# Two gate projections ahead of the mLSTM query/key projection, and the small loads released by an earlier load

## Chip, cores and metric

One core of one Trainium2 chip. The metric is the time of one execution in microseconds (us), and lower is better. The kernel is written out engine by engine: TensorE (matmuls), VectorE, ScalarE, GpSimd and SyncE each have a list of instructions of their own, and wait for each other on semaphores only.

## The reference, cut to what matters

One step of a two-layer diffusion trunk over 128 context and 256 latent tokens (T = 384), width 1024. The change lies in the first mixer of layer 0:

```
sh1, sc1, g1, sh2, sc2, g2 = split(silu(cvec) @ ada_w[l] + ada_b[l])      # adaLN, 1024 x 6144 per layer
h = rmsnorm(x) * (1 + sc1) + sh1
proj = h @ rec_w_in
qa, ka, va, ra, qb, kb, vb, ob, gk_lr, mg = split(proj)                   # 256 256 512 512 256 256 512 512 32 16
glog = log_sigmoid(gk_lr @ gla_gk_w + gla_gk_b) / 16                      # gates of the GLA heads
ig, lf = mg + mlstm_gate_b                                                # gates of the mLSTM heads
out_a = gla_scan(qa, ka, va, glog, state_gla); out_b = mlstm_scan(qb, kb, vb, ig, log_sigmoid(lf), state_mlstm_*)
x = x + g1 * (concat(norm(out_a) * silu(ra), norm(out_b) * sigmoid(ob)) @ rec_w_out)
```

Behind it follow a mixture of 16 experts, layer 1 (a long convolution, adaLN as well) and a second mixture of experts. All of it is in fp32.

## The kernel before

**Weights.** All large weights pass through `ring`, six slots of 2 MB. SyncE issues the loads of the list `order` one after the other (`load`, L607); a load into a slot first waits until the last use of what was in the slot is over. The order of this stretch: x and the position table (2.5 MB), adaLN loads 0 to 3 of layer 0 (slots 0 to 3), rec_w_in blocks 0, 3, 1, 4 (slots 4, 5, 0, 1), then adaLN loads 4 to 11 alternately in slots 2 and 3, then those of layer 1. A block of rec_w_in gives four query/key products: block 0 is `qka` (query and key of the GLA heads), block 3 `qkb` (those of the mLSTM heads).

**Small loads.** GpSimd issues them on its own queue (L728 to L762). It waits until slot 2 has been loaded twice, which is adaLN load 4, then issues five loads of `wg` (the 32 columns of gk and the 16 of mg, cut out of rec_w_in, L732 and L736), 23 small ones counted by `rec_small_loaded` (L740 to L755: gate weights and biases, norms, the cached states), waits until `mg` is computed, since the table `trec` lies in the same memory as `wg`, loads `trec` (L757), then eight small loads of the router's weights for both layers (L759 to L762), clears `A_sb`, which lies in ring slots 4 and 5, and from there clears `x_rows` in DRAM by a DMA of 5 MB (L766).

**TensorE.** `wide(key, ...)` (L1859) is one product of 128 weight columns (32 for gk) with all 384 tokens, eight steps of the inner dimension. `ada_mm(l, j)` (L1802) is a group of matmuls on adaLN load j, and four groups make one pair of adaLN rows. `ada_tr(l, pair)` (L1774) transposes the rows of a pair, once ScalarE has copied them (`ada_rows`, L935), and VectorE's `ada_cols` (L1207) brings them into place, which also frees the bank for the next pair. The order of this stretch is written out by hand: qka 0 to 3, group 4, then qkb 0, group 5, qkb 1, group 6, qkb 2, group 7, qkb 3, gk, transpose of pair 1, groups 8 and 9, mg, group 10, glog (a small product on gk), group 11, and then the products of va, vb, ra and ob (L1781), with groups of layer 1 between them.

**PSUM.** `claim` hands out the banks in turn, in the order in which the keys are claimed. VectorE and ScalarE share the copies out of them: ScalarE takes qka and qkb 0 and 1 (L976, L979) and the adaLN rows, VectorE qka and qkb 2 and 3 (L1254, L1257), gk (L1260), mg (L1264 to L1268, the last of these waiting for the small loads) and `ada_cols`.

Of the kernel before, what the change touches and what calls it, by code (L numbers as in the profile page):

```python
# [26 lines left out]
T = LP + LS  # L27
# [82 lines left out]
def build(nc, A, O):  # L110

    ctx = ExitStack()
    with ctx:
# [5 lines left out]
        def S(name):  # L119

            if name not in semaphores:
                semaphores[name] = ctx.enter_context(nc.semaphore(name))
            return semaphores[name]
# [50 lines left out]
        def claim(key, bank=None, keep=()):  # L174

            if bank is None:
                while turn[0] % 8 in keep:
                    turn[0] += 1
                bank = turn[0] % 8
                turn[0] += 1  # L180
            bank_uses[bank] += 1
            jobs[key] = (bank, bank_uses[bank])
            return bank
# [4 lines left out]
        def bank(key):  # L188
            return ps[jobs[key][0]]
# [7 lines left out]
        def full(eng, key):  # L197

            b, use = jobs[key]
            eng.wait_ge(bank_full[b], use)  # L200
# [4 lines left out]
        def free(ins, key):  # L205
            ins.then_inc(bank_free[jobs[key][0]], 1)
# [21 lines left out]
        held = (ADA_BANK,)  # L228
        for m in range(4):
            claim(("qka", m), keep=held)  # L230
        for m in range(4):
            claim(("qkb", m), keep=held)
        claim("gk", keep=held)
        claim("mg", keep=held)
        for m in range(4):
            claim(("glog", m), keep=held)
        for n in ("va", "vb", "ra", "ob"):
# [14 lines left out]
        held = (ADA_BANK, 7)  # L252
# [151 lines left out]
        def loaded(eng, key):  # L404
            slot, use, _ = loads[key]
            eng.wait_ge(S(f"slot{slot}_loaded"), 16 * use)
            return ring[:, slot, :]
# [21 lines left out]
        qkb = a.get(4 * T).rearrange("p (m t) -> p m t", m=4)  # L429
# [3 lines left out]
        trec = a.get(10 * P)  # L433
        mneg = [trec[:, 0:512], trec[:, 512:1024]]
        amask = [trec[:, 1024:1152].bitcast(U32), trec[:, 1152:1280].bitcast(U32)]
        wg = trec.rearrange("p (k n) -> p k n", k=DC)
# [281 lines left out]
        def _(pool):  # L718
            def clear(ap, name):
                pool.memset(ap, 0.0).then_inc(S(name), 1)  # L720
# [4 lines left out]
            clear(g36, "g36_cleared")  # L725
            clear(mcol, "mcol_cleared")
            pool.memset(vb[:, :, :, DV:DV + 1], 1.0).then_inc(S("vb_ones"), 1)
            pool.wait_ge(S("slot2_loaded"), 32)  # L728
            pool.wait_ge(S("wg_cleared"), 1)
            w_in = A["rec_w_in"][0].rearrange("(k p) n -> p k n", p=P)  # L730
            base = w_in.shape[2] - 16
# [19 lines left out]
            for d in range(2):  # L751
                for kc in range(2):
                    pool.dma_start(S0[:, d, kc, :], A["state_gla"][0, 0, d, 2 * kc:2 * kc + 2].rearrange("h k v -> (h k) v")).then_inc(S("rec_small_loaded"), 16)
                    pool.dma_start(C0[:, d, kc, 0:DV], A["state_mlstm_c"][0, 0, d, 2 * kc:2 * kc + 2].rearrange("h k v -> (h k) v")).then_inc(S("rec_small_loaded"), 16)
                    pool.dma_start(C0[:, d, kc, DV:], A["state_mlstm_n"][0, 0, d, 2 * kc:2 * kc + 2].rearrange("h (k o) -> (h k) o", o=1)).then_inc(S("rec_small_loaded"), 16)  # L755
            full(pool, "mg")
            pool.dma_start(trec, A["t_rec"]).then_inc(S("rec_tables_loaded"), 16)  # L757
            for l in range(2):
                pool.dma_start(wr[:, :, l, 0:NG], A["moe_w_group"][l].rearrange("(k p) n -> p k n", p=P)).then_inc(S("router_loaded"), 16)  # L759
                pool.dma_start(wr[:, :, l, NG:], A["moe_w_router"][l].rearrange("(k p) n -> p k n", p=P)).then_inc(S("router_loaded"), 16)  # L760
                pool.dma_start(b20[:, l, 0:NG], A["moe_b_group"][l].partition_broadcast(P)).then_inc(S("router_loaded"), 16)
                pool.dma_start(b20[:, l, NG:], A["moe_b_router"][l].partition_broadcast(P)).then_inc(S("router_loaded"), 16)  # L762
            clear(A_sb, "A_cleared")
            pool.wait_ge(S("zeros_cleared"), 1)
            for a0, p_, n in ((0, P, ROWS // P), (ROWS // P * P, ROWS % P, 1)):
# [139 lines left out]
        def _(act):  # L905
# [22 lines left out]
            def ada_rows(l, pair):  # L928

                full(act, ("adam", l, pair))  # L930
                if l or pair:
                    full(act, ("adac", l - (pair == 0), (pair - 1) % 3))
                if pair == 2 or l and pair == 0:
                    act.wait_ge(S("mod_rows_stored"), 32 * (l + (pair == 2)))
                free(act.copy(adar, bank(("adam", l, pair))[:]), ("adam", l, pair))  # L935
                if pair == 1:
                    evacuated(act, ("adam", l, pair))
                    for hf in range(2):
                        act.dma_start(shift_dram[l, :, hf * 512:(hf + 1) * 512], adar[64 + 32 * hf:66 + 32 * hf, :]).then_inc(S("mod_rows_stored"), 16)
                if l == 1 and pair == 2:  # L940
                    evacuated(act, ("adam", l, pair))
                    for hf in range(2):
                        act.dma_start(gate_dram[:, hf * 512:(hf + 1) * 512], adar[64 + 32 * hf:66 + 32 * hf, :]).then_inc(S("mod_rows_stored"), 16)
# [30 lines left out]
            for m in range(2):  # L974
                full(act, ("qka", m))
                free(act.activation(qka[:, m, :], bank(("qka", m))[:, 0:T], ACT.Copy, scale=DK ** -0.5), ("qka", m))  # L976
            for m in range(2):
                full(act, ("qkb", m))
                free(act.activation(qkb[:, m, :], bank(("qkb", m))[:, 0:T], ACT.Copy, scale=DK ** -0.5), ("qkb", m))  # L979
            ada_rows(0, 1)  # L980
            ada_rows(0, 2)

            for m in range(4):
# [195 lines left out]
        def _(v):  # L1179
# [19 lines left out]
            def ada_cols(l, pair):  # L1199

                key = ("adac", l, pair)
                at = V_ADA + l * NMOD * DC + 2 * DC * pair
                full(v, key)
                rows = bank(key)[:].rearrange("p (m q r) -> p m q r", m=4, q=4)[:, :, :, 0:2]
                bias = vecT[:, at:at + 2 * DC].rearrange("p (q m) -> p m q", m=4).unsqueeze(3)
                out = ada[:, l, 2 * DC * pair:2 * DC * (pair + 1), :].rearrange("p (q m) v -> p m q v", m=4)
                free(v.tensor_tensor(out, rows, bc(bias, [P, 4, 4, 2]), ALU.add), key)  # L1207
# [44 lines left out]
            for m in range(2, 4):  # L1252
                full(v, ("qka", m))
                free(v.tensor_copy(qka[:, m, :], bank(("qka", m))[:, 0:T]), ("qka", m))  # L1254
            for m in range(2, 4):
                full(v, ("qkb", m))
                free(v.tensor_copy(qkb[:, m, :], bank(("qkb", m))[:, 0:T]), ("qkb", m))  # L1257
            full(v, "gk")
            v.wait_ge(S("gkw_cleared"), 1)
            free(v.tensor_copy(gkT, bank("gk")[0:32, 0:T]), "gk")  # L1260
            ada_cols(0, 1)
            full(v, "mg")
            v.wait_ge(S("g36_cleared"), 1)
            v.tensor_copy(g36[:, 0, :], bank("mg")[0:36, 0:T])  # L1264
# [1 line left out]
            v.wait_ge(S("mlstm_f"), 1)  # L1266
            v.wait_ge(S("rec_small_loaded"), 16 * REC_SMALL)
            free(v.tensor_scalar(g36[:, 0, :], g36[:, 0, :], mcol[0:36, 0:1], None, ALU.add), "mg")  # L1268
            for m in range(DC):
                u_ready(v, "rec", m)  # L1270
            for m in range(4):
# [456 lines left out]
            for st, (c, od) in enumerate(STAGES):  # L1728
# [21 lines left out]
                for q in ((1, 2, 0) if od == 0 else range(4)):  # L1750
# [5 lines left out]
                    else:  # L1756
                        m = 4 * c + q
# [10 lines left out]
        def _(pe):  # L1768
# [25 lines left out]
            def ada_mm(l, j):  # L1794

                key, two = ("adam", l, j // 4), j % 4
                w = loaded(pe, ("ada", l, j)).rearrange("p (k n) -> p k n", k=2)
                if two == 0:
                    opened(pe, key)
                for k in range(2):  # L1800
                    for q in range(4):
                        ins = pe.matmul(bank(key)[32 * q:32 * q + 32, :], silc[:, 2 * two + k, :], w[:, k, q * 512:(q + 1) * 512],  # L1802
                                        start=(two == 0 and k == 0), stop=(two == 3 and k == 1))
                if two == 3:
                    done(ins, key)
                else:
                    ins.then_inc(S("ada_halves"), 1)

            def ada_tr(l, pair):

                evacuated(pe, ("adam", l, pair))
                transposes(("adac", l, pair), [(m * P, adar[:, m * P:(m + 1) * P]) for m in range(4)])
# [40 lines left out]
            def wide(key, w, rows=P, fresh=None):  # L1853

                opened(pe, key)
                for k in range(DC):
                    if fresh is not None:
                        u_ready(pe, fresh, k)
                    ins = pe.matmul(bank(key)[0:rows, 0:T], w(k), uT[:, k, :], start=(k == 0), stop=(k == DC - 1))  # L1859
                done(ins, key)  # L1860
# [16 lines left out]
            for m in range(4):  # L1877
                wide(("qka", m), lambda k: w[:, k, m * P:(m + 1) * P], fresh="rec" if m == 0 else None)
            ada_mm(0, 4)
            w = loaded(pe, ("rec", 3)).rearrange("p (k n) -> p k n", k=DC)  # L1880
            for m in range(4):
                wide(("qkb", m), lambda k: w[:, k, m * P:(m + 1) * P])
                if m < 3:
                    ada_mm(0, 5 + m)
            pe.wait_ge(S("wg_loaded"), 16 * 5)
            wide("gk", lambda k: wg[:, k, 0:32], 32)
            ada_tr(0, 1)
            ada_mm(0, 8)
            ada_mm(0, 9)
            wide("mg", lambda k: wg[:, k, 32:160])  # L1890
            ada_mm(0, 10)
            evacuated(pe, "gk")
            pe.wait_ge(S("rec_small_loaded"), 16 * REC_SMALL)
            for m in range(4):
# [477 lines left out]
```

## Time and profile before

| | us |
|---|---|
| median of 3 runs | 1322.21 |
| lowest, highest | 1312.7, 1322.69 |
| the profiled execution | 1312.7 |
| its span in the trace | 1310.9 |
| TensorE busy in it | 1172.2 (89%) |

The profiled execution is the fastest of the three. Its span, from the first instruction to the last, leaves 1.8 us of the execution's time outside. Times in the rows are counted from the start of the span. "Idle before" is the time in which an engine stood still ahead of an instruction, and the name behind the arrow is what released it.

### The profile page before, as it was taken

Reading aid. Unit: us, or ns where it says so; the run is one execution under the profiler, and the core shown is the slowest. Engines: PE = TensorE matmul, PEld = TensorE weight load, DVE = VectorE, ACT = ScalarE, POOL = GpSimd, SP = SyncE. Lnnn points to the kernel's source line nnn. Section 1 sums busy time; section 2 is a strip of 40 time slices with the busy share of each in tenths; the row PEclk is TensorE's granted clock in tenths of the full one; section 3 lists DMA queues with packets and bytes.
Section 4 is the critical chain, followed back from the end, with each engine's and each line's share of the span. In section 5 each row is a group of like instructions: output and inputs, shape, how many; then the busy total and the mean of one; then the engine's idle time right before and its main releaser. Section 6 shows DMA issues by size and latency. Waiting matters only on the chain.

```text
span 1310.9 us, 24682 instructions
## 1 busy us (share of the span) xinstructions
PE 1172.2 (89%) x10909; PEld 654.7 (50%) x10909; DVE 370.5 (28%) x919; ACT 215.4 (16%) x458; POOL 154.1 (12%) x167
## 2 busy tenths in 40 slices
PE   5999998868979998979988999998897999898984
PEld 2444333647565554545434665544565555454541
DVE  3104121473351110101156222575525111111103
ACT  2005001321131111111114111111012111011111
POOL 1223000022130000000010000142333000000001
PEclk9999999876989998999999999999998999899987
DMA  9979966502368999999946111001394999999964
GB/s 382 385 263 383 392 233 257 201 9 74 118 253 309 390 386 402 384 392 400 392 137 252 65 64 64 0 20 45 118 364 149 365 390 388 399 378 403 401 251 153
DMA packets 74875, 341.22 MB, mean 260 GB/s; under 512 B 6802, under 2 KB 17841, under 8 KB 59980
## 3 DMA queue, kind: packets, MB, share of 16 engines
q1 hardware_dynamic: 63032, 301.24, 59.4%
q0 software_dynamic: 11248, 37.99, 8.4%
q8 instruction: 89, 1.46, 0.4%
q10 hardware_dynamic: 484, 0.35, 0.1%
q14 instruction: 22, 0.18, 0.0%
HBM read 315.02 MB, written 24.54 MB: 259 GB/s over the span
## 4 chain that ended last, share of the span: by engine, by line
PE 71%; DMA 18%; DVE 6%; issue 3%; POOL 1%; ACT 1%; SPq 1%; DVEq 0%; POOLq 0%; ACTq 0%
PE ps L2141 18%; PE ps L1859 16%; PE ps L1781 16%; DMA ring<-in_moe_w_up 14%; PE ps L2163 7%; DMA ring<-in_ada_w 3%; PE ps L1802 3%; PE ps L2320 2%; PE ps L2151 1%; PE ps L1774 1%; PE ps L2291 1%; PE ps L2076 1%; PE ps L2124 1%; PE ps L1820 1%; DVE ring L1370 1%
## 5 line engine op out<-in xcount | busy, mean ns | idle before, releaser
L2141 PE MATMUL ps<-ring,work 128*32 128x256 f32 x5248 | 329.7, 395 | 43.5 <-DMA ring<-in_moe_w_up 39.2
L2141 PEld LDWEIGHTS ps<-ring,work 128*32 128x32 f32 x5248 | 165.1, 113 | 154.3 <-issue 60.0
L1859 PE MATMUL ps<-uT,ring 128*128 128x384 f32 x640 | 212.7, 488 | 2.5 <-DVE uT L1249 1.3
L1859 PEld LDWEIGHTS ps<-uT,ring 128*128 128x128 f32 x640 | 118.8, 190 | 86.9 <-issue 7.4
L2163 PE MATMUL ps<-ring,work 128*32 128x256 f32 x2624 | 156.3, 379 | 0.8 <-DVE work L1639 0.8
L2163 PEld LDWEIGHTS ps<-ring,work 128*32 128x32 f32 x2624 | 84.6, 110 | 57.3 <-DVE work L1639 1.1
L1639 DVE COPY work<-ps 128x128 f32<-128x128 f32 x82 | 23.9, 291 | 264.2 <-PE ps L2151 264.2
L1781 PE MATMUL ps<-ring,uT 128*128 128x512 f32 x192 | 85.3, 597 | 0.0
L1103 ACT ACTIVATE work<-ps 128x128 f32<-128x128 f32 x82 | 22.8, 278 | 364.2 <-PE ps L2141 364.2
L1635 DVE TENSOR_TENSOR work<-ps,work 128x128 f32<-128x128 f32 x82 | 23.9, 292 | 176.0 <-ACT work L1103 176.0
L845 POOL DMA_DIRECT2D work<-x_rows x30 | 15.6, 519 | 425.2 <-PE ps L2124 415.5
L1713 DVE SCALAR_TENSOR_TENSOR work<-ps,vecT,work 128x127 f32<-128x127 f32 x96 | 35.6, 412 | 89.4 <-ACT work L1157 88.5
L1781 PEld LDWEIGHTS ps<-ring,uT 128*128 128x128 f32 x192 | 35.5, 190 | 47.7 <-issue 47.7
L1781 PE MATMUL ps<-work 128*128 128x96 f32 (+1 forms) x176 | 53.5, 476 | 5.7 <-DVE work L1497 3.3
L1802 PE MATMUL ps<-ring,silc 128*32 128x512 f32 x384 | 48.7, 631 | 10.4 <-DMA ring<-in_ada_w 9.2
L1781 PE MATMUL ps<-work,ring 128*128 128x128 f32 (+3 forms) x256 | 43.2, 314 | 10.0 <-POOL ring L888 9.5
L1109 ACT COPY work<-ps 128x256 f32<-128x256 f32 x82 | 30.5, 372 | 121.9 <-PE ps L2163 121.9
L1781 PEld LDWEIGHTS ps<-work 128*128 128x128 f32 x176 | 32.2, 238 | 26.4 <-issue 26.4
L1781 PEld LDWEIGHTS ps<-work,ring 128*128 128x128 f32 (+1 forms) x256 | 36.2, 211 | 17.7 <-issue 11.3
L2320 PE MATMUL ps<-uT,ring 128*128 128x384 f32 x128 | 43.3, 491 | 0.9 <-DVE uT L1759 0.9
L881 POOL TENSOR_TENSOR ring<-ring 128x1024 f32<-128x1024 f32 x4 | 13.6, 3404 | 214.1 <-DVE ring L1736 214.1
L1774 PE MATMUL ps<-tab_common,work 128*128 128x128 f32 (+2 forms) x155 | 25.8, 308 | 11.8 <-DMA work<-in_t_pos 10.8
(317 smaller groups left out, 1008.4 us busy)
## 6 DMA issues: line engine op xcount, KB each, us to landing
ring<-in_moe_w_down SPq DMA_DIRECT2D x32, 2048.0 KB, 16.1
ring<-in_moe_w_gate SPq DMA_DIRECT2D x32, 2048.0 KB, 13.2
ring<-in_moe_w_up SPq DMA_DIRECT2D x32, 2048.0 KB, 16.6
ring<-in_ada_w SPq DMA_DIRECT2D x24, 2048.0 KB, 11.4
ring<-in_rec_w_in SPq DMA_DIRECT2D x6, 2048.0 KB, 24.1
ring<-in_hy_w_in SPq DMA_DIRECT2D x6, 2048.0 KB, 10.7
y_rows<-work SPq DMA_DIRECT2D x72, 96.0 KB, 12.6
work<-x_rows POOLq DMA_DIRECT2D x16, 384.0 KB, 7.8
```

The lines of the kernel that those rows point to most:

```text
L1103: act.activation(sg[:, (FIRST[p] + i) % 2, :], bank((l, p, "GU", i))[:, 0:P], ACT.Silu).then_inc(S("silu_out"), 1)
L1109: free(act.copy(ysb[:, p % 2, i, :], bank((l, p, "Y", i))[:, 0:256]), (l, p, "Y", i))
L1635: free(v.tensor_tensor(hh[:, par, :], bank((l, p, "GU", i))[:, P:2 * P], sg[:, par, :], ALU.mult), (l, p, "GU", i))
L1639: free(v.tensor_copy(hT[:, (FIRST[p] + i) % 2, :], bank((l, p, "HT", i))[:, 0:P]), (l, p, "HT", i))
L1713: ins = v.scalar_tensor_tensor(dst[:, a0 + do:a0 + do + n], src[:, a0 + so:a0 + so + n], w, dst[:, a0 + do:a0 + do + n], ALU.mult, ALU.add)
L1774: ins = pe.transpose(bank(key)[0:n, at:at + p], src, ident[0:p, 0:p])
L1781: ins = pe.matmul(out, lhsT, rhs, start=(i == 0), stop=(i == n - 1))
L1802: ins = pe.matmul(bank(key)[32 * q:32 * q + 32, :], silc[:, 2 * two + k, :], w[:, k, q * 512:(q + 1) * 512], start=(two == 0 and k == 0), ...
L1859: ins = pe.matmul(bank(key)[0:rows, 0:T], w(k), uT[:, k, :], start=(k == 0), stop=(k == DC - 1))
L2141: ins = pe.matmul(bank(key)[32 * q:32 * q + 32, 0:2 * P].rearrange("p (a n) -> p a n", a=2), xg[:, u, k, 32 * i:32 * i + 32], ring[:, 3 * ...
L2163: ins = pe.matmul(bank(key)[32 * q:32 * q + 32, 0:256], hT[:, (FIRST[p] + i) % 2, 32 * k:32 * k + 32], ring[:, n, at:at + 256], start=(k = ...
L2320: ins = pe.matmul(bank(("ho", m))[:, 0:T], w[:, k, (m % 4) * P:(m % 4 + 1) * P], uT[:, k, :], start=(k == 0), stop=(k == DC - 1))
```

## The change

gk and mg are computed ahead of qkb, and their banks are claimed in that order. The adaLN groups and the transpose of pair 1 are dealt out anew among the products: gk, group 5, mg, group 6, qkb 0, group 7, transpose, qkb 1, group 8, qkb 2, group 9, qkb 3, group 10, glog, group 11. The copies of ScalarE and VectorE follow this order. GpSimd's small loads wait for the first load of slot 3 (adaLN load 3) in place of the second of slot 2 (adaLN load 4). The eight router loads come ahead of the wait for mg and of the table, and the clearing of `A_sb` and `x_rows` waits for qkb 3. Nothing is added or taken away in what is computed or loaded.

```diff
         for m in range(4):
             claim(("qka", m), keep=held)
+        claim("gk", keep=held)
+        claim("mg", keep=held)
         for m in range(4):
             claim(("qkb", m), keep=held)
-        claim("gk", keep=held)
-        claim("mg", keep=held)
...
-            pool.wait_ge(S("slot2_loaded"), 32)
+            pool.wait_ge(S("slot3_loaded"), 16)
...
-            full(pool, "mg")
-            pool.dma_start(trec, A["t_rec"]).then_inc(S("rec_tables_loaded"), 16)
             for l in range(2):
                 pool.dma_start(wr[:, :, l, 0:NG], ...)   # four router loads a layer
+
+            full(pool, "mg")
+            pool.dma_start(trec, A["t_rec"]).then_inc(S("rec_tables_loaded"), 16)
+            full(pool, ("qkb", 3))
             clear(A_sb, "A_cleared")
...
+            ada_rows(0, 1)
             for m in range(2):
                 full(act, ("qkb", m))
                 free(act.activation(qkb[:, m, :], bank(("qkb", m))[:, 0:T], ACT.Copy, scale=DK ** -0.5), ("qkb", m))
-            ada_rows(0, 1)
             ada_rows(0, 2)
...
-            for m in range(2, 4):
-                full(v, ("qkb", m))
-                free(v.tensor_copy(qkb[:, m, :], bank(("qkb", m))[:, 0:T]), ("qkb", m))
             full(v, "gk")
...
-            ada_cols(0, 1)
             full(v, "mg")
...
             free(v.tensor_scalar(g36[:, 0, :], g36[:, 0, :], mcol[0:36, 0:1], None, ALU.add), "mg")
+            ada_cols(0, 1)
+            for m in range(2, 4):
+                full(v, ("qkb", m))
+                free(v.tensor_copy(qkb[:, m, :], bank(("qkb", m))[:, 0:T]), ("qkb", m))
...
             ada_mm(0, 4)
+            pe.wait_ge(S("wg_loaded"), 16 * 5)
+            wide("gk", lambda k: wg[:, k, 0:32], 32)
+            ada_mm(0, 5)
+            wide("mg", lambda k: wg[:, k, 32:160])
+            ada_mm(0, 6)
             w = loaded(pe, ("rec", 3)).rearrange("p (k n) -> p k n", k=DC)
             for m in range(4):
                 wide(("qkb", m), lambda k: w[:, k, m * P:(m + 1) * P])
-                if m < 3:
-                    ada_mm(0, 5 + m)
-            pe.wait_ge(S("wg_loaded"), 16 * 5)
-            wide("gk", lambda k: wg[:, k, 0:32], 32)
-            ada_tr(0, 1)
-            ada_mm(0, 8)
-            ada_mm(0, 9)
-            wide("mg", lambda k: wg[:, k, 32:160])
-            ada_mm(0, 10)
+                ada_mm(0, 7 + m)
+                if m == 0:
+                    ada_tr(0, 1)
             evacuated(pe, "gk")
```

## Rows read from the trace of the kernel before

**Rows 1.** The page: the chain that ended last, shares by engine.
```profile
PE 71%; DMA 18%; DVE 6%; issue 3%; POOL 1%; ACT 1%; SPq 1%; DVEq 0%; POOLq 0%; ACTq 0%
```
**Rows 2.** TensorE's timeline: start, duration (us), line, operation, count [idle before <- releaser].
```profile
31.46 3.32 PE L1802 MATMUL ps<-ring,silc 128*32 128x512 f32 x16 [3.46 <-DMA ring<-in_ada_w]
35.56 0.63 PE L1774 MATMUL ps<-tab_common,work 128*128 128x128 f32 x4 [0.78 <-ACT work L935]
37.48 20.88 PE L1859 MATMUL ps<-uT,ring 128*128 128x384 f32 x64 [1.29 <-DVE uT L1249]
...
58.29 1.92 PE L1802 MATMUL ps<-ring,silc 128*32 128x512 f32 x16
...
87.14 5.35 PE L1859 MATMUL ps<-uT,work 128*32 128x384 f32 x16
...
93.44 3.64 PE L1802 MATMUL ps<-ring,silc 128*32 128x512 f32 x32 [0.37 <-DVE ada L1207]
...
102.84 1.92 PE L1802 MATMUL ps<-ring,silc 128*32 128x512 f32 x16 [0.39 <-DMA ring<-in_ada_w]
...
108.28 1.92 PE L1802 MATMUL ps<-ring,silc 128*32 128x512 f32 x16 [0.74 <-DMA ring<-in_ada_w]
110.13 7.13 PE L1781 MATMUL ps<-ring,uT 128*128 128x512 f32 x16
...
219.85 3.45 PE L1802 MATMUL ps<-ring,silc 128*32 128x512 f32 x16 [4.59 <-DMA ring<-in_ada_w]
```
**Rows 3.** SyncE's issues: adaLN loads 4, 5 and 8, and load 0 of layer 1.
```profile
38.83 5.29 SPq L607 DMA_DIRECT2D ring<-in_ada_w  x1
...
44.17 1.23 SPq L607 DMA_DIRECT2D ring<-in_ada_w  x1
...
74.70 0.37 SPq L607 DMA_DIRECT2D ring<-in_ada_w  x1
...
104.82 0.37 SPq L607 DMA_DIRECT2D ring<-in_ada_w  x1
```
**Rows 4.** The DMA view, the same four loads in order: KB, us to landing.
```profile
ring<-in_ada_w SPq DMA_DIRECT2D x1, 2048.0 KB, 19.2
...
ring<-in_ada_w SPq DMA_DIRECT2D x1, 2048.0 KB, 19.0
...
ring<-in_ada_w SPq DMA_DIRECT2D x1, 2048.0 KB, 11.0
...
ring<-in_ada_w SPq DMA_DIRECT2D x1, 2048.0 KB, 13.9
```
**Rows 5.** Timeline: first projection's weight load, and GpSimd's first and last issues.
```profile
37.45 0.30 PEld L1859 LDWEIGHTS ps<-uT,ring 128*128 128x128 f32 x2 [1.50 <-DMA ring<-in_rec_w_in]
...
58.34 1.09 POOL L732 DMA_DIRECT2D work<-in_rec_w_in  x1 [53.13 <-DMA ring<-in_ada_w]
...
74.41 0.54 POOL L755 DMA_DIRECT2D work<-in_state_mlstm_n  x1
...
103.27 0.91 POOL L759 DMA_DIRECT2D wr<-in_moe_w_group  x1
...
108.45 0.55 POOL L762 DMA_DIRECT2D b<-in_moe_b_router  x1
```
**Rows 6.** The DMA view, 58 to 82 us: GpSimd's queue, its slowest small loads.
```profile
q0 software_dynamic: 896, 0.88, 18.5%
...
work<-in_state_mlstm_n POOLq DMA_DIRECT2D x4, 0.5 KB, 8.0
```
**Rows 7.** The windows view: us, engines busy (x), then PEclk, DMA share, GB/s.
```profile
55.00:58.00 3.00, 3.00 (x11) 1.69 (x9) 0.00 (x0) 0.00 (x0) 0.00 (x0) 1.00 1.03 429
60.00:76.00 16.00, 16.00 (x73) 7.65 (x70) 0.00 (x0) 0.98 (x2) 14.95 (x27) 1.00 1.01 296
```
**Rows 8.** The windows view about group 11 of layer 1, 219.85 us.
```profile
219.80:221.00 1.20, 1.15 (x8) 0.40 (x12) 0.00 (x0) 0.00 (x0) 0.00 (x0) 0.50 1.01 430
...
223.20:226.00 2.80, 2.54 (x30) 1.93 (x28) 1.15 (x2) 0.00 (x0) 0.00 (x0) 1.00 1.00 395
```

## The prediction

> **What bounds the kernel now.** I read the page first. The chain that ended last is 71% TensorE and 18% DMA [rows 1], so a microsecond added to TensorE's order of work, or to a load that it waits for, is a microsecond of the kernel. The change lies between 37 and 110 us, so the next view is TensorE's timeline there [rows 2]. Look at what is missing: from 37.48 us (first query/key projection) to 102.8 us there is no wait of TensorE worth a name except 0.37 us on VectorE at 93.44. Then come 0.39 us before adaLN group 10 and 0.74 us before group 11, both on a load of in_ada_w. From 110.13 us on no wait is shown until 219.85.
>
> The third view is the queue of the loads [rows 3, 4]. The loads of SyncE are taken up one after the other: adaLN load 4, issued at 38.83, lands 19.2 us later, at 58.0; load 5, issued at 44.17, lands at 63.2. TensorE begins on load 4 at 58.29 [rows 2], when its last projection before it (20.88 us from 37.48) has just ended, at 58.36 by the chain's reckoning: load 4 has 0.2 to 0.3 us to spare. The weight load of the first projection at 37.45 was released by in_rec_w_in [rows 5], so rec 0 has next to none either. TensorE is never seen waiting here, and still the loads are as tight as they can be. This is the place to watch.
>
> The fourth view is GpSimd's own queue [rows 5]. It sits for 53.13 us until adaLN load 4 has landed, and issues its 28 small loads from 58.34 to 74.95 us (16.6 us). Then it waits for mg, and issues the table in_t_rec and, from 103.27 to 109.00, eight router loads (5.7 us).
>
> **The change, part by part.**
>
> (a) GpSimd waits for slot 3's first load (adaLN 3) instead of slot 2's second (adaLN 4). TensorE starts on load 3 at 31.46 after a wait for it [rows 2], so GpSimd starts at 31.5. With the same 16.6 us it is through its 28 small loads at 48.1; the eight router loads no longer stand behind the wait for mg, and follow until 53.8. All of them now go while rec 0, rec 3, rec 1, rec 4 and adaLN 4 are queued on SyncE, and the load that TensorE needs next, adaLN 4, is last of them. The small loads do not queue behind these: before, they landed up to 8 us after issue, while the large ones took 11 to 19 [rows 4, 6]. So nearly all of their cost now falls ahead of adaLN 4.
>
> What do they cost? Before, they ran between 60 and 76 us. There the engines were as busy as ever (1.01) but moved 296 GB/s, against 429 from 55 to 58 [rows 7]. That is 16 us x 133 GB/s = 2.1 MB not moved, plus the 0.88 MB that the small loads themselves carried [rows 6]: 3.0 MB at 429 GB/s, 7.0 us. Landing times say the same: from load 5 (63.2) to load 8 (74.70 + 11.0 = 85.7) pass 22.5 us for three loads that take 5.2 each (63.2 - 58.0), 6.9 us too many, and the engines had work in hand all the while [rows 3, 4, 7].
>
> The router loads: adaLN load 0 of layer 1, issued at 104.82, lands at 118.7 [rows 3, 4]; behind load 11, used at 108.28 [rows 2], it should land at 113.4. Of the 5.3 us too many, 1.5 belong to the table (0.655 MB at 429) and a little to the clearing of x_rows. Bounds 0 and 5.3 us; I take 3.5, since their packets are as short as those of the mg columns.
>
> So adaLN 4 lands 10.5 us later, at 68.5 (bounds: nothing, if these losses were not of bandwidth, and 12.3). If rec 0 is the one that is held up first, the projection starts later, but the wait at adaLN 4 shrinks by as much. TensorE's new wait is 10.5 - 0.2 = 10.3 us. Behind it in TensorE's order stands everything: gk, mg, qkb.
>
> By the Trainium skill, page "DMA: Bandwidth & Descriptors", section "Why small descriptors are slow (HBM only)", a packet has a fixed overhead of about 3 cycles over its beats of 32 bytes. Counting from the code some 11,700 descriptors, at 5 cycles or less each, over 16 engines at the 850 MHz that the same page gives, is an estimate of 4.3 us instead of 10.5; by it the sum below would be +4.8 us, 1327 us. The rows show more than that for the 28 loads alone.
>
> (b) After such a wait TensorE's clock is low. The group of 16 adaLN matmuls takes 1.92 us at the full clock; after the wait of 3.46 us it takes 3.32, and after 4.59 us 3.45, at a granted clock of 0.50 (1.2 GHz) which is over at 223.2 [rows 2, 8]. +1.4 us. Upper bound: gk (5.35 us, [rows 2]) too runs at half speed, +5.4; nothing speaks for it, since the clock was back within one such group both times.
>
> (c) gk and mg ahead of qkb: the same wide products (5.35 us for gk, about as much for each other one) and the same adaLN groups, none added: 0. Group 8 now comes before the second half of qkb, so slot 2 is freed one product earlier relative to the rest: load 10 is issued some 12.5 us before its use (two products of 5.35 and one group of 1.92), against one product and one group, 7.3 us, before; load 11 is issued some 10 us before its use (product, group, and 2.8 us of glog) as before, but load 10 is no longer ahead of it. The waits of 0.39 and 0.74 us go, and the wait of 0.37 us on VectorE too, as a product now stands between the transpose and group 8: -1.5 us.
>
> (d) The transpose of the adaLN rows now comes straight behind group 7, and has to wait for ScalarE's copy. Before, this one followed two products and waited for nothing; the like of it at 35.56 waited 0.78 us [rows 2]. +0.8 us. Behind it stands the second qkb product. ScalarE is free, as its adaLN copy now stands ahead of its two qkb copies.
>
> (e) VectorE's and ScalarE's copies are the same in number. VectorE's mg copy waits for the small loads, which are in by about 62; mg is not ready before 80. The qkb copies come last and are asked for only by banks of va and the mLSTM, far behind. The banks of glog and va keep their numbers. The table comes after mg, over 100 us ahead of the masks. All 0; were the mg copy late, only group 8's bank would feel it.
>
> (f) The clearing of x_rows now starts before group 11 rather than behind it: at the worst its load shares bandwidth in its last microseconds, 0 to 1 us; I take 0.
>
> Sum: +10.3 + 1.4 - 1.5 + 0.8 = +11.0 us. From 110.13 us on nothing in TensorE's chain depends on a load issued earlier than its own release, so the shift goes through to the end. Against the profiled execution (1312.7 us, span 1310.9) it makes 1323.7. That execution lies 9.5 us under the median of the three runs; against the median, 1322.2, it makes 1333.2 us, 0.83% slower. I forecast 1333.
>
> **Rivals.**
> 1. The small loads cost nothing where they now run, the queue being deep there. Then only -1.5 + 0.8 is left: 1321.5 us, faster by a hair. For it: the two losses are inferred from rates. Against it: the landings give the same number. It decides if adaLN 4 lands by 59.
> 2. Short packets are cheap next to the rec loads. The landing times of loads 6 to 8 count in part because only one or two loads were queued there. If half of 7.0 is such a gap and the routers cost 1: 4.5 - 0.2 + 1.4 - 0.7 = +5.0, 1327. It decides below about 6 us of loss. (The Trainium skill's page "DMA: Bandwidth & Descriptors" with its 3 cycles would speak for this case, but the landings of loads 5 and 8 bear it out only in part.)
> 3. The stall is larger: routers 5.3, and gk at half clock: 12.1 + 6.8 - 0.7 = +18, 1340, slower by over 1%. Against it: the clock rows.
> 4. The shift is given back behind 110 us, 1322. It would need a wait on something that did not move; the 4.59 us at 219.85 is for a load that TensorE itself released shortly before. Nothing speaks for it.
>
> **How the numbers follow.** Forecast (+8 to +13): 0.5. Rival 1: 0.1; rival 2: 0.2; rival 3 or anything above +13: 0.15; rival 4: 0.05. The runs before spread over 10 us, so some of it blurs the edge of 1% (13.2 us), which is about what a measurement of this kernel can tell from no change. Slower by over 1%: rival 3 and the upper edge of the forecast, 0.25. Faster by over 1%: no mechanism gives it, 0.03 for scatter. Within 1%: 0.72. The range of 8 in 10 leaves out the lower part of rivals 1 and 4 and the top of 3: 1320 to 1341.
>
> **What would show it.** GpSimd's first issue at 31.5 instead of 58.34. A new wait of TensorE of some 10 us ahead of adaLN 4's matmuls near 59, released by in_ada_w, and that group at 3.3 us instead of 1.92. Between 34 and 60 us a rate near 300 GB/s instead of 400. No wait at groups 10 and 11; 0.8 us before the second adaLN transpose, released by ScalarE. The first va product at about 121 instead of 110.13. If adaLN 4 lands on time, (a) is wrong and all else with it; if the wait is there but va still starts near 110, the sum is wrong.

## The result

| | kernel before | changed kernel |
|---|---|---|
| median of 20 runs, us | 1315.35 | 1323.83 |
| lowest to highest | 1312.56 to 1322.69 | 1317.84 to 1329.36 |
| the profiled execution | 1312.7 | 1325.53 |

The changed kernel is slower: ratio 1.0055, interval 1.0041 to 1.0070, or 7.2 us at 1315 us (the two medians lie 8.5 us apart). The forecast was a loss of 11.0 us from the same mechanism, and a time of 1333 us. Direction and mechanism are borne out. The size of the loss was put half as large again, and the time came out 9 us lower, most of it because the kernel before is faster than the median from which the forecast counted.

TensorE's timeline of the changed kernel, in the columns of [rows 2]; lines are shifted by two, so that an adaLN group is L1804 and a wide product L1861:

```profile
36.87 22.60 PE L1861 MATMUL ps<-uT,ring 128*128 128x384 f32 x64 [1.90 <-DMA ring<-in_rec_w_in]
67.22 3.64 PE L1804 MATMUL ps<-ring,silc 128*32 128x512 f32 x16 [7.74 <-DMA ring<-in_ada_w]
...
93.49 0.63 PE L1776 MATMUL ps<-tab_common,work 128*128 128x128 f32 x4 [0.80 <-ACT work L937]
...
113.63 1.92 PE L1804 MATMUL ps<-ring,silc 128*32 128x512 f32 x16
...
118.26 1.92 PE L1804 MATMUL ps<-ring,silc 128*32 128x512 f32 x16
120.11 7.13 PE L1783 MATMUL ps<-ring,uT 128*128 128x512 f32 x16
```

In what follows "va" is the start of the first va product, TensorE's milestone behind the changed stretch. The second row is the new wait, 7.74 us for adaLN load 4, with its group at half the clock (3.64 us for 1.92). The third is the wait of 0.80 us for ScalarE. Groups 10 and 11 wait for nothing. va starts at 120.11, where the profile of before had 110.13.

GpSimd's first issue, SyncE's issue of load 4 and its time to landing (timeline and DMA view of the changed kernel):

```profile
31.87 1.09 POOL L732 DMA_DIRECT2D work<-in_rec_w_in  x1 [26.66 <-DMA ring<-in_ada_w]
...
42.50 7.78 SPq L607 DMA_DIRECT2D ring<-in_ada_w  x1
...
ring<-in_ada_w SPq DMA_DIRECT2D x1, 2048.0 KB, 24.7
```

Load 4 lands at 67.2 us instead of 58.0 [rows 3, 4]. Why is in the windows view (columns as in [rows 7]):

```profile
30.00:36.00 6.00, 2.55 (x20) 0.84 (x20) 3.52 (x10) 0.59 (x1) 4.13 (x5) 1.00 1.04 386
36.00:42.00 6.00, 5.13 (x11) 2.89 (x12) 4.22 (x15) 0.00 (x0) 6.00 (x12) 0.72 1.11 207
42.00:54.00 12.00, 12.00 (x39) 7.11 (x38) 0.00 (x0) 0.98 (x2) 12.00 (x21) 1.00 1.06 347
54.00:60.00 6.00, 5.47 (x17) 2.87 (x16) 1.05 (x2) 0.00 (x0) 0.50 (x1) 1.00 1.08 239
60.00:66.00 6.00, 0.00 (x0) 0.00 (x0) 0.07 (x1) 0.00 (x0) 0.00 (x0) 0.63 1.04 426
```

Two of these windows in the kernel before, where no small load runs in them:

```profile
36.00:42.00 6.00, 4.71 (x16) 2.76 (x15) 5.10 (x18) 0.00 (x0) 0.00 (x0) 1.00 1.05 387
54.00:60.00 6.00, 6.00 (x30) 2.70 (x28) 0.56 (x1) 0.00 (x0) 1.66 (x2) 1.00 1.01 421
```

The engines are shown busy throughout (1.04 to 1.11), but the rate falls twice: to 207 GB/s instead of 387 while the wg loads with their rows of 128 and of 16 bytes run, and to 239 instead of 421 while the router loads (rows of 16 and 64 bytes) run. The 23 loads between them, most of their bytes in rows of 512, take less away (347 instead of 397). In the last window TensorE has no matmul at all.

### The profile page after: what moved, and what is told of

It is laid out like the page before. It is cut to its first block, busy times and chain, and to the rows that moved or that the text cites. A ratio compares the mean times of both kernels' runs of the same rounds, so it can differ in the third digit from the quotient of the medians.

```text
span 1323.7 us, 24682 instructions
## 1 busy us (share of the span) xinstructions
PE 1181.5 (89%) x10909; PEld 661.5 (50%) x10909; DVE 370.5 (28%) x919; ACT 215.3 (16%) x458; POOL 155.0 (12%) x167
## 4 chain that ended last, share of the span: by engine, by line
PE 73%; DMA 15%; DVE 6%; issue 2%; SPq 2%; POOL 1%; ACT 1%; DVEq 0%; POOLq 0%; ACTq 0%
PE ps L2142 19%; PE ps L1783 16%; PE ps L1861 15%; DMA ring<-in_moe_w_up 12%; PE ps L2164 7%; PE ps L1804 3%; DMA ring<-in_ada_w 2%; PE ps L2321 2%; PE ps L1776 2%; PE ps L2152 1%; PE ps L2125 1%; PE ps L2292 1%; PE ps L2077 1%; SPq L607 1%; PE ps L1822 1%
## 5 line engine op out<-in xcount | busy, mean ns | idle before, releaser
L1861 PE MATMUL ps<-uT,ring 128*128 128x384 f32 x640 | 214.3, 492 | 2.9 <-DMA ring<-in_rec_w_in 1.9
L1861 PEld LDWEIGHTS ps<-uT,ring 128*128 128x128 f32 x640 | 119.9, 192 | 87.2 <-issue 7.8
L1804 PE MATMUL ps<-ring,silc 128*32 128x512 f32 x384 | 51.5, 654 | 16.0 <-DMA ring<-in_ada_w 15.2
L847 POOL DMA_DIRECT2D work<-x_rows x30 | 15.6, 520 | 424.1 <-PE ps L2125 414.6
## 6 DMA issues: line engine op xcount, KB each, us to landing
y_rows<-work SPq DMA_DIRECT2D x72, 96.0 KB, 12.4
```

## The experiments

One point of method first. Each unprofiled time is compared with runs of the kernel before on the same chip, and va is read from the one profile of each kernel. The four later profiles of the kernel before, which serve as the measure of va, are of another chip than the other runs; the changed kernel's va on three chips lies between 119.93 and 120.58. None leaves out any work; the busy delay alone adds some, which it throws away.

### Which part costs: the trigger, the router loads, the wg loads

**The trigger alone**, in the kernel before:

```diff
-            pool.wait_ge(S("slot2_loaded"), 32)
+            pool.wait_ge(S("slot3_loaded"), 16)
```

> The kernel before with one thing altered: GpSimd's small loads are released by adaLN load 3 instead of load 4; products, groups and router loads stay where they were. Theory A: load 4 lands some 6.9 us late, TensorE waits about 6.7 us for it and its group takes 3.6 instead of 1.92; va starts near 118.5, the time is 6 to 8 us above the kernel before. Theory B (the order of products costs the time): no slower than before by more than 2 us.

Measured: ratio 1.0051 (1.0032 to 1.0070), va at 117.70, and in its timeline

```profile
64.39 3.21 PE L1802 MATMUL ps<-ring,silc 128*32 128x512 f32 x16 [3.29 <-DMA ring<-in_ada_w]
```

By the time, one line of the change makes nearly all of the loss (6.7 of 7.3 us); by va it is 4.2 of 6.7 (table below). Load 4 is 6.3 us late. TensorE's wait is only 3.29 us, not 6.7: its products before it ended later than in the profile of before, in 23.75 us instead of 20.88, for a reason that comes up below.

**The router loads back behind the table**, in the changed kernel:

```diff
-            for l in range(2):
-                (four router loads)
             full(pool, "mg")
             pool.dma_start(trec, A["t_rec"]).then_inc(S("rec_tables_loaded"), 16)
+            for l in range(2):
+                (four router loads)
             full(pool, ("qkb", 3))
```

> The changed kernel with the eight router loads back behind the wait for mg and the table. Theory A with packets of 16 bytes as the dear ones (the rate fell to 181 to 277 GB/s while the router loads ran, 2.3 us lost): load 4 lands 2 to 3 us earlier than 67.2, TensorE's wait falls from 7.74 to about 5.3 us, va at about 117.7. If only the bytes of the router loads count (0.18 MB, 0.4 us), the wait stays at 7.3.

Measured: ratio 1.0006 (0.9979 to 1.0032), va at 117.12. Its timeline, and its rate in the window in which the changed kernel had 239:

```profile
64.45 3.64 PE L1803 MATMUL ps<-ring,silc 128*32 128x512 f32 x16 [4.82 <-DMA ring<-in_ada_w]
```
```profile
54.00:60.00 6.00, 5.63 (x18) 3.03 (x16) 0.89 (x2) 0.00 (x0) 0.00 (x0) 1.00 1.06 409
```

Load 4 lands 2.8 us earlier, as expected from short packets; the 0.18 MB of the router loads would be 0.4 us. One thing stays open here: this kernel and the one with the trigger alone hold load 4 up alike (64.4 us) and reach va within 0.6 us of each other, yet on the same chip their ratios are 1.0006 and 1.0051, with intervals that touch only at their ends.

**Only wg early**, from the kernel just shown:

```diff
             pool.wait_ge(S("gkw_cleared"), 1)
+            pool.wait_ge(S("slot2_loaded"), 32)
             for d in range(2):
                 pool.dma_start(gkw[...], ...)
```

> The changed kernel with only the five loads of wg released by adaLN load 3; the other 23 small ones wait for adaLN load 4 as before, and the router loads go behind the table. Theory A, with the short packets as the dear ones: the four mg loads of 16 bytes a packet cost about 2.8 us ahead of load 4, the 512-byte rows of the states none: TensorE waits 1.5 to 3 us, va at 111.5 to 113.5, ratio 0.998 to 1.002. If the bytes count alone, wg (0.19 MB) costs 0.5 us and TensorE waits 0.3.

Measured: ratio 0.9996 (0.9968 to 1.0024), va at 112.11.

```profile
61.48 1.92 PE L1804 MATMUL ps<-ring,silc 128*32 128x512 f32 x16 [1.13 <-DMA ring<-in_ada_w]
```

Load 4 is used at 61.48 upon landing, 3.4 us later than the 58.0 of before, for 0.19 MB that by their bytes are 0.5 us. The wait is a little shorter than the 1.5 to 3 us expected. With the three kernels the delay of 9.2 us is taken apart: wg 3.4, the other 23 small loads 3.0 (61.4 to 64.4), the router loads 2.8 (64.4 to 67.2). The loss against the kernel before is gone within the interval.

**The trigger put back**, with all else of the change:

```diff
-            pool.wait_ge(S("slot3_loaded"), 16)
+            pool.wait_ge(S("slot2_loaded"), 32)
```

> The changed kernel with GpSimd's small loads released by adaLN load 4 again, so that only the order of products, groups, router loads and the table is new. Theory A: load 4 lands at 58 as before and its group does not wait, but the five loads of wg, issued from 58.4 to 63, land near 70, and gk waits for them for 9 to 10 us with a low clock behind it: va at 120 to 122, time as the changed kernel's or 1 to 2 us above. If wg could have come that late for nothing, va would be at 109.5 and the time at 1315.

> The fourth experiment once more (small loads released by load 4 again). Its va was at 120.34, where the changed kernel's is, but its ratio 1.0017 (0.9992 to 1.0042) below that kernel's. Theory A: scatter, 1.004 to 1.007 this time, as the changed kernel's. Rival: 1.002 again, so 3 to 5 us are given back when the wait falls on gk and not on group 4.

The first run had ratio 1.0017 (0.9992 to 1.0042), the second, beside the changed kernel, 1.0043 (1.0020 to 1.0066). The waits at gk in their two profiles:

```profile
69.78 6.68 PE L1861 MATMUL ps<-uT,work 128*32 128x384 f32 x15 [9.50 <-DMA work<-in_rec_w_in]
```
```profile
66.26 6.72 PE L1861 MATMUL ps<-uT,work 128*32 128x384 f32 x15 [3.29 <-DMA work<-in_rec_w_in]
```

So with gk ahead of qkb the earlier trigger is needed: without it the wait stands at gk instead of at group 4. The weights of gk landed 3.5 us apart in the two profiles though issued at the same time (58.41 and 58.46). What differs is adaLN load 6, which SyncE issues once group 4 has let go of slot 2. In the first profile that is at 60.34, in the midst of the wg loads, and the four loads of mg take 7.0 us to land. In the second the first products had run at a low clock (23.41 us for 20.88), load 6 comes at 63.03 only, and they take 4.1. So the later load in the queue is the likely cause; no run isolates it. The low first ratio was partly scatter; both intervals overlap.

### Is it the order of the loads that makes it a loss?

**rec_w_in blocks 1 and 4 behind adaLN loads 6 and 8**, in the changed kernel. They are wanted from va on (111 us) and vb on, and stood ahead of load 4:

```diff
-        for n, slot in enumerate((4, 5, 0, 1)):
+        for n, slot in ((0, 4), (1, 5)):
             add_rec(n, slot)
-        for j in range(4, 12):
+        for j in range(4, 7):
+            add_ada(0, j, 2 + j % 2)
+        add_rec(2, 0)
+        for j in range(7, 9):
+            add_ada(0, j, 2 + j % 2)
+        add_rec(3, 1)
+        for j in range(9, 12):
             add_ada(0, j, 2 + j % 2)
```

> The changed kernel with one thing altered: the loads of rec_w_in blocks 1 and 4, wanted only from 110 us on, go behind adaLN loads 6 and 8 instead of ahead of load 4. Theory A (the small loads cost bandwidth ahead of adaLN load 4, and TensorE's wait of 7.74 us for it is the whole loss): load 4 lands near 52, no wait at its group and none of the low clock behind it, first va product at about 109.5 us against 120.11 in the changed kernel and 110.13 in the kernel before; the time is that of the kernel before or up to 1 us less, about 1315. Theory B (the new order of products itself costs time behind 110 us): the wait goes, yet 5 us or more of the loss stay, about 1320 or more.

> The first experiment once more, beside the changed kernel on one chip. It had 0.9969 (0.9946 to 0.9992) where its first va product, at 111.5, gave no reason for a gain. Theory A: that was scatter, 0.998 to 1.002 this time, and 7 to 9 us below the changed kernel. Rival (a gain behind 110 us): 0.997 again.

Measured: 0.9969 (0.9946 to 0.9992), and on another chip 0.9967 (0.9944 to 0.9991). The wait at group 4 is gone, and load 7 is late by a little (timeline of the second):

```profile
59.43 1.92 PE L1810 MATMUL ps<-ring,silc 128*32 128x512 f32 x16
...
82.03 1.92 PE L1810 MATMUL ps<-ring,silc 128*32 128x512 f32 x16 [1.25 <-DMA ring<-in_ada_w]
...
111.38 7.13 PE L1789 MATMUL ps<-ring,uT 128*128 128x512 f32 x16
```

This version beats both kernels: 4 us below the kernel before, twice, and 1311.85 against 1323.21 us for the changed kernel on one chip. The expectation of 0.998 to 1.002 was missed and its rival's number, 0.997, came again. Half of the gain is the va of this kernel against later profiles of the kernel before (below); the other half stays open. The first expectation had missed too: it had put va at 109.5 and foreseen no new wait, which load 7 now has.

**The same load order in the kernel before:**

> The kernel before with the load order of the first experiment alone (rec_w_in blocks 1 and 4 behind adaLN loads 6 and 8). Its loads were in time to within 0.2 us already, so nothing but the waits of 0.39 and 0.74 us can change: within 1 us of the kernel before, ratio 0.999 to 1.001. If the gain of 4 us that the first experiment showed (0.9969) came from the load order and not from the order of the products, it is here too: 0.997.

Measured: 1.0001 (0.9975 to 1.0026), va at 112.69. Alone it is worth nothing.

**Both repairs together** (this load order, only wg early, router loads late):

> The changed kernel with both repairs: the load order of the first experiment, and only the five wg loads released by adaLN load 3, the other small ones by load 4, the router loads behind the table. Theory A: no wait for any load from 60 to 120 us, va at 109 to 111.5 us; the waits of the kernel before at groups 8, 10 and 11 are gone and 0.8 us before the transpose is new: 0.5 to 1 us below the kernel before, ratio 0.998 to 1.001. If the new order of products gives something back behind 110 us (rival B turned round), 3 to 5 us below: ratio 0.996.

Measured: 1.0025 (1.0000 to 1.0051), va at 117.91. This is outside the expected 0.998 to 1.001, and worse than the load order alone:

```profile
84.88 1.92 PE L1810 MATMUL ps<-ring,silc 128*32 128x512 f32 x16 [2.49 <-DMA ring<-in_ada_w]
...
102.58 1.92 PE L1810 MATMUL ps<-ring,silc 128*32 128x512 f32 x16 [1.98 <-DMA ring<-in_ada_w]
```

Two waits take the place of one. The 23 small loads are not the reason: they are issued from 51.19 to 63.2 us, when SyncE's queue is nearly empty:

```profile
54.00:60.00 6.00, 6.00 (x21) 3.48 (x20) 0.56 (x1) 0.00 (x0) 6.00 (x12) 1.00 0.29 59
```

The router loads are issued from 76 to 81.6 us and so fall ahead of loads 7 to 9, which in this order have blocks 1 and 4 ahead of them as well. In the kernel of the first experiment they run early, while nothing is needed soon. Of the 6.5 us by which va is later than there, the waits are 3.2. The rest is TensorE's clock: the first products took 23.49 us instead of 22.58 and began 0.7 us later, and group 11 ran at half the clock (3.55 us) without a wait before it.

### Does a delay before 110 us reach the end?

**A busy delay**: in the kernel before, the fourth qka product is computed twice more and thrown away.

```diff
             for m in range(4):
+                if m == 3:
+                    opened(pe, ("qka", 3))
+                    for _ in range(2):
+                        for k in range(DC):
+                            pe.matmul(bank(("qka", 3))[:, 0:T], w[:, k, 3 * P:4 * P], uT[:, k, :], start=(k == 0), stop=(k == DC - 1))
                 wide(("qka", m), ...)
```

> The kernel before with two more computations of the fourth qka product, thrown away: TensorE is held up for 10.7 us ahead of adaLN group 4, at work and so at the full clock, and no load is slowed. Theory A (what is lost before 110 us goes through to the end): va near 120, 9 to 11 us above the kernel before, a ratio near 1.0075. Rival (part of a delay is given back behind, where the stretches of experts run at the pace of their loads): 3 to 7 us, ratio 1.002 to 1.005.

Measured: 1.0113 (1.0071 to 1.0156), 9 to 21 us, va at 124.86. The delay was 10.7 us by design; it reaches the end in full, and the rival of 3 to 7 us falls. Both va and the time are above what was expected (near 120, and 9 to 11 us), va because the expectation counted from 110.13.

**The changed kernel again**, on two more chips:

> The changed kernel once more, unaltered, beside the kernel before on the chip of the other three. If its loss is the wait that it shows: va at about 120 as in its first profile, ratio near 1.0055 again (1.003 to 1.008).

> The changed kernel unaltered, as the measure for the other three on this chip: ratio 1.004 to 1.007, va at 120 to 121.

Measured: 1.0057 (1.0030 to 1.0083) with va at 120.58, and 1.0055 (1.0031 to 1.0079) with va at 119.93. So va is 10 us later than in [rows 2], three times, the time only 7.3 us longer, three times, and yet a delay goes through whole. One of the numbers had to be wrong.

**Four more profiles of the kernel before:**

> The kernel before, unaltered, one more profile. Theory A (the profile on which the prediction rested was of a quick execution, 1312.7 us where 20 runs have a median of 1315.35): the first qka products take 22.6 us or more instead of 20.88, because the clock is low at their start, and va starts at 111.5 to 113.5. Rival (the changed kernel gets back 2 to 3 us behind 110 us): va at 110.1 here too.

> The kernel before, unaltered, as the run before this one: va between 111.5 and 113.5 us by theory A, 110.1 by the rival.

> The kernel before, unaltered, as the run before this one: va between 111.5 and 113.5 us by theory A, 110.1 by the rival.

> The kernel before, unaltered, as the run before this one: va between 111.5 and 113.5 us by theory A, 110.1 by the rival.

| profile of the kernel before | time | first 64 qka matmuls | group 4 at | group 11 | va at |
|---|---|---|---|---|---|
| of the prediction | 1312.7 | 20.88 | 58.29 | 1.92 | 110.13 |
| 1 | 1315.56 | 22.60 | 59.52 | 1.92 | 112.42 |
| 2 | 1315.82 | 22.60 | 59.38 | 3.56 | 113.30 |
| 3 | 1317.12 | 23.31 | 60.95 | 3.64 | 115.47 |
| 4 | 1318.33 | 22.60 | 59.46 | 3.23 | 112.67 |

The third of them, its timeline:

```profile
37.71 23.31 PE L1859 MATMUL ps<-uT,ring 128*128 128x384 f32 x64 [1.29 <-DVE uT L1249]
...
96.10 3.64 PE L1802 MATMUL ps<-ring,silc 128*32 128x512 f32 x32 [0.37 <-DVE ada L1207]
...
105.94 1.92 PE L1802 MATMUL ps<-ring,silc 128*32 128x512 f32 x16 [0.83 <-DMA ring<-in_ada_w]
...
111.89 3.64 PE L1802 MATMUL ps<-ring,silc 128*32 128x512 f32 x16 [1.26 <-DMA ring<-in_ada_w]
```

Three of the four lie in the expected 111.5 to 113.5, the third above it. The mean of va in the four is 113.5 us, that of the changed kernel's three 120.2: 6.7 us apart, where the runs say 7.3. With the prediction's profile counted in, the mean is 112.8 and the difference 7.4. From va to the end of the span the five profiles of the kernel before take 1199.8 to 1203.8 us and the changed kernel's three 1203.0 to 1205.2, so no gift shows behind va either; one of 2 us or less would be lost in this scatter.

The profile on which the prediction rested was of the quickest kind of execution. In the others the first products begin at a low clock (0.50 to 0.65 of it from 37 to 41 us in profile 1, 1.00 in that of the prediction) and take 22.6 us or more instead of 20.88, and group 11 runs at half the clock in three of four. It stands behind a short wait for load 11, but that does not decide it: in profile 1 the wait is 1.07 us and the group takes 1.92, and in the second profile of the changed kernel it is slow without one:

```profile
117.48 3.17 PE L1804 MATMUL ps<-ring,silc 128*32 128x512 f32 x16
```

Measured from 113.5 us, va agrees with nearly all of the ratios:

| kernel | va - 113.5 | measured, us at 1316 |
|---|---|---|
| changed (mean of three) | +6.7 | +7.3 |
| trigger alone | +4.2 | +6.7 (4.2 to 9.2) |
| router loads late | +3.6 | +0.8 (-2.8 to 4.2) |
| trigger back, first | +6.8 | +2.2 (-1.1 to 5.5) |
| trigger back, again | +3.4 | +5.7 (2.6 to 8.7) |
| both repairs | +4.4 | +3.3 (0 to 6.7) |
| only wg early | -1.4 | -0.5 (-4.2 to 3.2) |
| loads first, in before | -0.8 | +0.1 (-3.3 to 3.4) |
| loads first | -2.1 | -4.2 (two runs: -7.4 to -1.1) |
| busy delay | +11.4 | +14.9 (9.3 to 20.5) |

Only the first run of the trigger put back lies outside, and its repetition doesn't. Each va but the first is of one profile, and such a position scatters by some us, as the four above show. That the loads-first kernel is 2 us better than its va accounts for is inside its interval and stays open, as does the difference between the second row and the third.

## Why the prediction was right or wrong

Two steps failed. The slack of load 4 and, with it, the other waits of the kernel before were read from one quick execution, which made the sum 4 us too high. And the reference point, 1322.2 us, was 6.9 us above the 1315.35 of 20 runs; that is the larger part of the 9 us by which the forecast time is off.

**(a) the cost of the small loads: right in kind, a little high.** The delay of load 4 was put at 10.5 us and is 9.2. The 28 loads were put at 7.0 and cost 6.4 (3.4 + 3.0). The router loads were put at 3.5 and cost 2.8. Rival 2, 4.5 us in all, falls. So does the 4.3 us worked out from the Trainium skill's "DMA: Bandwidth & Descriptors", section "Why small descriptors are slow (HBM only)". Its count of 5 cycles or less is too small for the rows of 128 and 512 bytes; with the beats of every row the same rule gives an estimate of 5.3 us. The direction of that rule agrees with the two dips, but its overhead of 3 cycles a packet gives well under the 9.2 us measured. Rival 1, no cost, falls too.

**(a) the slack of load 4: the step that failed.** "0.2 to 0.3 us to spare" was read from an execution in which TensorE reached group 4 at 58.29. In the four later profiles it reached it at 59.38 to 60.95, so the slack is 1.4 to 2.9 us, mean 1.8. A landing is fixed by the queue and TensorE's arrival is not: in all five profiles load 4 lands 19.2 us after its issue. On average the changed kernel is therefore held up by 67.2 - 59.8 = 7.4 us at group 4, and not by 10.3. Of the 2.9 us between them 1.6 are the slack and 1.3 the cost of the loads; together they are the larger part of the 4 us that the sum was too high.

**(b) the low clock behind the wait: right, a little low.** Put at +1.4, it is 1.7, 1.5 and 1.7 for the group in the three profiles (3.64, 3.39 and 3.64 us for 1.92). gk lost up to 0.6 behind it (15 matmuls in 5.60 us, where the kernel with only wg early has 5.00). Together that is +1.9 on average. The upper bound of rival 3 wasn't reached.

**(c) the waits that go: undersized.** Put at -1.5. All three did go. In the four later profiles they amount to 0.38 + 0.60 + 0.94 = 1.9 us on average, and a wait for load 7, in two of them, to 0.2 more. Group 11 ran at half the clock in three of them, 1.2 on average, but also in one of the changed kernel's three profiles, 0.4: that makes -2.9 us. Of it 0.8 is the draw of the clock at group 11, which no run ties to the change. The same profile as in (a) hid all this, its group 11 having waited 0.74 us and yet run at 1.92. The products and groups themselves, put at 0, are 0.5 us shorter in the new order: without waits and low clock, group 4 to va is 50.3 to 50.4 us in the four profiles and 49.8 in the three.

**(d) the wait for ScalarE: right**, 0.80 us in each of the profiles, as put.

**(e), (f):** nothing of the copies, the banks or the clearing shows up as a wait before 120 us.

**Anew:** +7.4 + 1.9 - 2.9 - 0.5 + 0.8 = +6.7 us. This is the difference in va taken apart, so it has to come out at 6.7; the runs, which are independent of it, have 7.3.

**The passage to the end: right.** Rival 4 falls with the busy delay. In the first profile of the changed kernel va is 10.0 us late, the output projection of layer 0's mixer 15.6 us late, and the last matmuls of the first expert stage 11.2 (677.45 and 666.27). The step up is the clock again; the step down is the scatter of the expert stage, for which that profile takes 344.9 us, the changed kernel's other two 347.3 and 350.3, and the five of the kernel before 345.9 to 349.3. The step up: the stage of the A products (keys with queries of the GLA heads, and group 11 of layer 1 behind them; the group at 219.85 us ahead of them is group 10, not 11 as rows 8 have it), 7.4 us long in before, took 12.4 at a granted clock of 0.51 instead of 1.00 (windows view, before and changed):

```profile
223.20:230.70 7.50, 6.93 (x70) 4.18 (x68) 4.38 (x6) 0.00 (x0) 0.00 (x0) 1.00 1.03 388
```
```profile
233.70:246.20 12.50, 11.93 (x68) 7.13 (x64) 4.37 (x6) 0.00 (x0) 0.00 (x0) 0.51 1.04 390
```

Of the changed kernel's other two profiles one has 12.4 us there and the other 7.4; of the four later ones of before, one has 12.6 and three 7.4 to 7.6. With all kernels of this document it is slow in 3 of 8 profiles with the old order of products and in 3 of 10 with the new, so it is a draw of each execution and not part of the change.

**The reference point.** The forecast of 1333 was put on a median of 1322.2 from three runs, and 20 runs have 1315.35: 6.9 us of its error. The sum itself was made against the one profile of 1312.7, and the text noted that this was 9.5 us under the median, but used it only to move the total. The gap said more: that the profile's waits and slacks were those of a quick execution.

## What to carry to other kernels

A load that comes just in time without a visible wait is the thing to look for before anything is moved ahead of it in the queue; here 0.9 MB of small loads, moved 26 us earlier, and 0.2 MB of router weights held up the one load that mattered by 9.2 us. Price small loads by the bandwidth that is missing while they run and not by their bytes, and put what is wanted late behind what is wanted soon, so that there is room for them: in this kernel that turned a loss of 7 us into a gain of 4. And count a forecast from as many runs as can be had: the median of three was off by as much as the whole effect. A slack read from one profile needs a second one, above all if its execution is at the edge of the runs: here the landing of load 4 repeats to 0.2 us, and TensorE's arrival at it varies by 2.7.

## What the runs showed of the hardware

- Loads in short rows cost about seven times what their bytes would: wg (0.19 MB, of which 0.06 in rows of 16 bytes and the rest in rows of 128) 3.4 us and the router loads (0.18 MB) 2.8 us of a queue that moves 387 to 429 GB/s, with the engines shown busy at 1.11 and 1.08. Which of the row sizes, 16, 64 or 128 bytes, is the dear one was not isolated. The 23 loads with most of their 0.69 MB in rows of 512 bytes cost 3.0 us, not quite twice their bytes, in a stretch of 347 GB/s.
- GpSimd's loads don't wait for the backlog of SyncE's: they landed about 5 to 7 us after issue while 2 MB loads took 22 to 34 in the same stretch.
- The same instructions of the same kernel took 20.88, 22.60 or 23.31 us for 64 matmuls, and 7.4 or 12.6 us for the stage of the A products, by where TensorE's granted clock was low. The stage stands behind a wait of TensorE for a load and a group at half the clock each time. It took 12.4 us in the changed kernel's first profile behind a wait of 4.96 us, but 12.6 in a profile of before behind one of 4.59 and 7.4 in another behind the same 4.59; what decides between the two stays open.
- The clock can be low without a wait just before it: group 11 took 3.17 and 3.55 us for 1.92 in two profiles where TensorE had not stood still ahead of it.
